# Seven fast products in another order, one block load fewer for each, and the short chunk second

## The reference

```python
h = rmsnorm(x, attn_norm)
proj = einsum('bsd,de->bse', h, w_in)          # 4352 columns
out_a = dilated_attention(qa, ka, va, slopes_a)
out_b = swa_sink_attention(qb, kb, vb, slopes_b, sinks)
mix = concatenate([rmsnorm(out_a, out_norm_a), rmsnorm(out_b, out_norm_b)], axis=-1)
x = x + einsum('bse,ed->bsd', mix, w_out)
h = rmsnorm(x, ffn_norm)
gate = einsum('bsd,df->bsf', h, w_gate)        # 5632 columns
up = einsum('bsd,df->bsf', h, w_up)
x = x + einsum('bsf,fd->bsd', silu(gate) * up, w_down)
return rmsnorm(x, final_norm)
```

## The kernel before

| product | weight operand | made in |
|---|---|---|
| P1 | near left | y, loaded |
| P5 | near right - near left | x = x - y (DVE, `f_sum`) |
| P6 | far right - P5's | x = z - x (`f_sum`) |
| P7 | far right - near right | y = z - y (`f_sum`), after y was loaded with near right a second time |
| P3 | far right | z |
| P4 | P6's operand - far left | x = x - z (`f_sum`), after z was loaded with far left |
| P2 | far left | z |

## Time and profile before

### The profile page before, as it was taken

How to read it: one execution, slowest core, us unless ns; L and a number is a source line. 1 busy time by engine, 2 the same in 40 slices (tenths; PEclk the granted TensorE clock), 3 DMA queues, 4 the chain that set the end, 5 groups by cost and what they waited for, 6 DMA issues and landing times.

```text
span 2030.3 us, 29105 instructions
## 1 busy us (share of the span) xinstructions
PE 1956.6 (96%) x10132; PEld 1668.6 (82%) x10132; DVE 1736.3 (86%) x2397; ACT 1258.9 (62%) x2238; POOL 169.2 (8%) x261
## 2 busy tenths in 40 slices
PE   9999999999999999999999999999997998999984
PEld 8888888888888988888888888888885776777763
DVE  8877677777767999999999999999997979879878
ACT  6566666675346555555555555555566887888864
POOL 4012323223000000000000000000000000000000
PEclk9999999999999999999999999999998999999987
DMA  9322222224334344444444444444465564464542
GB/s 341 119 84 74 68 69 72 69 73 151 94 114 155 127 136 135 135 135 135 131 139 135 136 135 135 135 135 135 135 223 181 187 218 141 150 222 150 168 145 83
DMA packets 133626, 279.30 MB, mean 138 GB/s; under 512 B 12592, under 2 KB 12624, under 8 KB 132608
## 3 DMA queue, kind: packets, MB, share of 16 engines
q1 hardware_dynamic: 121488, 242.27, 37.5%
q0 software_dynamic: 6640, 23.82, 3.0%
q10 hardware_dynamic: 5376, 11.56, 1.6%
HBM read 246.14 MB, written 31.46 MB: 137 GB/s over the span
## 4 chain that ended last, share of the span: by engine, by line
PE 75%; DVE 15%; DMA 4%; issue 3%; ACT 2%; SPq 0%; POOL 0%; ACTq 0%; POOLq 0%; DVEq 0%
PE bank L841 24%; PE bank L844 13%; PE bank L702 8%; PE bank L704 8%; PE bank L703 8%; DVE f_lo L1688 5%; DMA fast_z<-in_w_down 3%; PE bank L768 3%; PE bank L770 3%; PE bank L769 3%; PE bank L894 1%; DVE fast_y L2210 1%; DVE fast_x L2207 1%; DVE a_lo L1688 1%; PE bank L879 1%
## 5 line engine op out<-in xcount | busy, mean ns | idle before, releaser
L841 PE MATMUL bank<-s_two,t_hi 128*128 128x512 f32 x2352 | 557.3, 390 | 0.0
L1428 ACT ACTIVATE t_hi<-t_raw 128x1792 fp32r<-128x1792 f32 x176 | 302.7, 1721 | 360.4 <-DVE t_raw L2056 272.8
L841 PEld LDWEIGHTS bank<-s_two,t_hi 128*128 128x128 f32 x2352 | 433.5, 188 | 84.7
L2062 DVE TENSOR_TENSOR t_lo<-t_raw,t_hi 128x1792 fp32r<-128x1792 f32 x176 | 355.3, 2019 | 20.7 <-ACT t_hi L1428 20.1
L844 PEld LDWEIGHTS bank<-s_two,t_lo 128*128 128x128 f32 x2352 | 298.9, 191 | 10.6 <-DVE t_lo L2062 0.8
L844 PE MATMUL bank<-s_two,t_lo 128*128 128x256 f32 x2352 | 302.3, 283 | 0.4 <-DVE t_lo L2062 0.4
L702 PE MATMUL bank<-f_hi,a_hi 128*128 128x512 f32 x616 | 250.7, 407 | 52.2 <-DVE f_lo L1688 45.6
L703 PE MATMUL bank<-f_hi,a_lo 128*128 128x512 f32 x616 | 246.0, 399 | 0.0
L704 PE MATMUL bank<-f_lo,a_hi 128*128 128x512 f32 x616 | 245.8, 399 | 0.0
L2053 DVE TENSOR_TENSOR t_raw<-t_raw 128x1024 f32<-128x1024 f32 x176 | 214.7, 1220 | 19.2 <-DMA t_raw<-in_w_gu 17.5
L702 PEld LDWEIGHTS bank<-f_hi,a_hi 128*128 128x128 f32 x616 | 119.1, 193 | 92.6 <-DVE f_lo L1688 63.9
(11 more groups left out here) (233 smaller groups left out, 3413.5 us busy)
## 6 DMA issues: line engine op xcount, KB each, us to landing
t_raw<-in_w_gu SPq DMA_DIRECT2D x348, 256.0 KB, 2.8
raw<-in_w_in SPq DMA_DIRECT2D x104, 256.0 KB, 2.6
fast_y<-in_w_down SPq DMA_DIRECT2D x44, 512.0 KB, 4.4
fast_z<-in_w_down SPq DMA_DIRECT2D x44, 512.0 KB, 5.5
gu_mid<-part POOLq DMA_DIRECT2D x43, 512.0 KB, 2.9
...
```

The source lines that it names most:

```text
L841: mm = nc.tensor.matmul(b[:, :], t_hi[r][:, ti, q, :], both, start=d == 0 and q == 0, stop=d == DOUBLES - 1 and q == 1 and i < 4, skip_gro ...
L1428: nc.scalar.activation(t_hi[r][:, :, :, :].rearrange("p a q c -> p (a q c)"), t_raw[r][:, 1:8, :, :].rearrange("p a q c -> p (a q c)"), AC ...
L2062: nc.vector.tensor_tensor(t_lo[r][:, :, :, :].rearrange("p a q c -> p (a q c)"), t_raw[r][:, 1:8, :, :].rearrange("p a q c -> p (a q c)"), ...
```

## The change

The products P6 and P7 change places, so the order is P1, P5, P7, P6, P3, P4, P2, and the buffers are used so that each of the four blocks is loaded once:

| product | weight operand | made in |
|---|---|---|
| P1 | near left | y, loaded |
| P5 | near right - near left | y = x - y |
| P7 | far right - near right | x = z - x |
| P6 | far right - P5's | y = z - y |
| P3 | far right | z |
| P4 | P6's operand - far left | y = y - x, after x was loaded with far left |
| P2 | far left | x |

The load of far left into x is issued when `f_low` of P7 is done. The next chunk's blocks are issued after P3 (z), P4 (y) and P2 (x). The short chunk becomes the second (`DEPTHS = (2, 1, 2, 2, 2, 2)`), and the start and the end of the stage are rewritten for this: more tiles are gated before and in the first slots, the sums of group 43 (`post(7, 1)`) move from slot 1 to slot 4, the residual is loaded after the last chunk's P6 rather than in its P3, and its first add stands in slot 16.

The diff without the places of buffers and the counts that follow from the new order:

```diff
-P1, P5, P6, P7, P3, P4, P2 = range(FAST)
-SUMMED_W, SUMMED_A = (P5, P6, P7, P4), (P5, P6, P7, P3)
-FAST_FROM = "yxxyzxz"
+P1, P5, P7, P6, P3, P4, P2 = range(FAST)
+SUMMED_W, SUMMED_A = (P5, P7, P6, P4), (P5, P7, P6, P3)
+FAST_FROM = "yyxyzyx"
 FAST_BANK = (((0, 4), (6, 1)), ((2, 3), (5, 7)))
 CHUNKS = 6
 ENDING = CHUNKS - 1
-DEPTHS = (1,) + (2,) * ENDING
+DEPTHS = (2, 1, 2, 2, 2, 2)
...
+    def follows(c, u):
+
+        return min((d for d in range(c + 1, CHUNKS) if DEPTHS[d] > u), default=CHUNKS)
...
         sp.wait_ge(t_used, ALL_T - 3)
-        for k in (0, 1, 4, 5):
-            sp.wait_ge(gu_stored, 16 * (tile_of(0, k) + 1))
+        for k in range(2):
             load_gu(0, k)
         sp.wait_ge(t_used, ALL_T - 2)
         for h in range(2):
             load_block("y", 0, 0, h, 0, 0)
+        for k in (2, 3):
+            load_gu(0, k)
         sp.wait_ge(t_used, ALL_T - 1)
         for h in range(2):
+            load_block("y", 0, 1, h, 0, 0)
+        for k in (4, 5):
+            load_gu(0, k)
+        for h in range(2):
             load_block("x", 0, 0, h, 0, 1)
+        for k in (6, 7):
+            load_gu(0, k)
+        sp.wait_ge(t_used, ALL_T)
         for h in range(2):
-            load_block("z", 0, 0, h, 1, 1)
-        for k in (4, 5, 6, 7, 2, 3):
-            sp.wait_ge(gu_stored, 16 * (tile_of(1, k) + 1))
-            load_gu(1, k)
+            load_block("x", 0, 1, h, 0, 1)
+        for u in range(2):
+            for h in range(2):
+                load_block("z", 0, u, h, 1, 1)
         for v in range(len(UNITS)):
             c, p, u, h = UNITS[v]
             e = v - FIRST_UNIT[c]
-            if p == P5:
-                sp.wait_ge(f_lo_done, UNIT_AT[c, P1, u, h] + 1)
-                sp.wait_ge(f_sum_done, W_SUM[c, p, u, h])
-                load_block("y", c, u, h, 0, 1)
-            if p == P3:
+            if p == P7:
                 sp.wait_ge(f_lo_done, v + 1)
-                load_block("z", c, u, h, 1, 0)
-            if c < ENDING and p == P7:
+                load_block("x", c, u, h, 1, 0)
+            if p == P4 and follows(c, u) < CHUNKS:
                 sp.wait_ge(f_lo_done, v + 1)
-                load_block("y", c + 1, u, h, 0, 0)
-            if c < ENDING and p == P4:
+                load_block("y", follows(c, u), u, h, 0, 0)
+            if p == P2 and follows(c, u) < CHUNKS:
                 sp.wait_ge(f_lo_done, v + 1)
-                load_block("x", c + 1, u, h, 0, 1)
-            if c < ENDING and p == P2:
+                load_block("x", follows(c, u), u, h, 0, 1)
+            if p == P3 and follows(c, u) < CHUNKS:
                 sp.wait_ge(f_lo_done, v + 1)
-                load_block("z", c + 1, u, h, 1, 1)
-            if c == 0 and p == P4:
-                load_block("y", 1, 1, h, 0, 0)
-            if (c, p, h) == (0, P2, 0):
+                load_block("z", follows(c, u), u, h, 1, 1)
+            if (c, e) == (1, 0):
                 sp.wait_ge(gu_stored, 16 * TILES)
-            if c == 0 and p == P2:
-                load_block("x", 1, 1, h, 0, 1)
-            if (c, p, h) == (0, P2, 1):
-                sp.wait_ge(folded, TILES - 2)
-                for half in range(2):
-                    load_block("z", 1, 1, half, 1, 1)
-            if 0 < c < ENDING and e in range(4):
-                before = (c - 1, P2, DEPTHS[c - 1] - 1)
-                sp.wait_ge(a_lo_done, ITEM[before] + 1)
+            if c < ENDING and p == P1 and 4 + e in range(4, 4 + 2 * DEPTHS[c + 1]):
+                sp.wait_ge(gs_done, GATE[c, 5 + 2 * (DEPTHS[c] > 1)])
+                if c > 0:
+                    sp.wait_ge(a_lo_done, ITEM[c - 1, P2, DEPTHS[c - 1] - 1] + 1)
                 load_gu(c + 1, 4 + e)
-            if c < ENDING and p == P7 and h == 1:
-                sp.wait_ge(a_sum_done, A_SUM[c, P7, u])
+            if DEPTHS[c] == 1 and p == P1 and h == 1:
+                for k in (6, 7, 2, 3):
+                    load_gu(c + 1, k)
+            if c < ENDING and p == P6 and h == 1 and u < DEPTHS[c + 1]:
+                sp.wait_ge(a_sum_done, A_SUM[c, P6, u])
                 for k in (2 * u, 2 * u + 1):
                     load_gu(c + 1, k)
-            if (c, p, u, h) == (ENDING, P3, 0, 0):
-                sp.wait_ge(a_sum_done, A_SUM[c, P7, 1])
+            if (c, p, u, h) == (ENDING, P6, 1, 1):
+                sp.wait_ge(a_sum_done, A_SUM[c, P6, 1])
                 sp.wait_ge(a_lo_done, ITEM[c - 1, P2, 1] + 1)
                 for n in range(NC):
                     sp.wait_ge(x_moved[n], X_SPILLED)
...
-            if (c, e) == (ENDING, 17):
-                act.wait_ge(f_lo_done, UNIT_AT[c, P7, 1, 1] + 1)
+            if (c, e) == (ENDING, 21):
+                act.wait_ge(f_lo_done, UNIT_AT[c, P4, 1, 1] + 1)
                 act.dma_start(g_fin[:, :], final_norm.partition_broadcast(P)).then_inc(gfin_loaded, 16)
...
-        f_high(1)
         act.wait_ge(t_lo_done, ALL_T)
         a_high(ITEMS[0])
-        silu(0, 4)
-        silu(0, 5)
-        take_products(7, 1, 0, 5)
+        f_high(1)
+        silu(0, 2)
+        silu(0, 3)
+        take_products(7, 1, 0, 4)
         act.wait_ge(t_used, ALL_T - 1)
         f_high(2)
         a_high(ITEMS[1])
-        take_products(7, 1, 5, QUAD)
+        take_products(7, 1, 4, QUAD)
+        silu(0, 4)
+        silu(0, 5)
...
-                nc.vector.tensor_tensor(x, x, y, ALU.subtract).then_inc(f_sum_done, 1)
+                nc.vector.tensor_tensor(y, x, y, ALU.subtract).then_inc(f_sum_done, 1)
+            elif p == P7:
+                dve.wait_ge(fast_loaded["z", u][h], loads_of("z", c, u, h, 1))
+                nc.vector.tensor_tensor(x, z, x, ALU.subtract).then_inc(f_sum_done, 1)
             elif p == P6:
-                dve.wait_ge(fast_loaded["z", u][h], loads_of("z", c, u, h, 1))
                 dve.wait_ge(f_sum_done, W_SUM[c, P5, u, h])
-                nc.vector.tensor_tensor(x, z, x, ALU.subtract).then_inc(f_sum_done, 1)
-            elif p == P7:
-                dve.wait_ge(fast_loaded["y", u][h], loads_of("y", c, u, h, 2))
                 nc.vector.tensor_tensor(y, z, y, ALU.subtract).then_inc(f_sum_done, 1)
             else:
-                dve.wait_ge(fast_loaded["z", u][h], loads_of("z", c, u, h, 2))
-                nc.vector.tensor_tensor(x, x, z, ALU.subtract).then_inc(f_sum_done, 1)
+                dve.wait_ge(fast_loaded["x", u][h], loads_of("x", c, u, h, 2))
+                dve.wait_ge(f_sum_done, W_SUM[c, P6, u, h])
+                nc.vector.tensor_tensor(y, y, x, ALU.subtract).then_inc(f_sum_done, 1)
...
-            if e == 13:
+            if e == 16:
+                for n in range(NC):
+                    dve.wait_ge(x_moved[n], X_BACK)
+                dve.wait_ge(kept, kept_count(ENDING, P1, 1))
+                for h in range(2):
+                    add_block(sum_of(P1, h), 0, h, r2_sign, 0)
+            if e == 17:
                 dve.wait_ge(kept, kept_count(ENDING, P6, 1))
                 for h in range(2):
                     join(P6, P1, h, 0)
-            if e == 17:
-                dve.wait_ge(kept, kept_count(ENDING, P7, 1))
+            if e == 18:
                 for h in range(2):
                     join(P7, P6, h, h + 1)
-            if e == 18:
-                for h in range(2):
-                    join(P6, P5, h, 2)
...
+            if v in (0, 2):
+                gate_times_up(0, 4 + v)
+                gate_times_up(0, 5 + v)
...
             if v == 1:
+                gate_scaled(0, 6)
+                gate_scaled(0, 7)
+            if v == 4:
                 post(7, 1)
...
+        gate_scaled(0, 2)
+        gate_scaled(0, 3)
+        f_low(1)
+        gate_times_up(0, 2)
+        gate_times_up(0, 3)
+        f_low(2)
+        a_low(ITEMS[1])
         gate_scaled(0, 4)
         gate_scaled(0, 5)
-        f_low(1)
-        gate_times_up(0, 4)
-        gate_times_up(0, 5)
-        f_sum(2)
-        a_sum(ITEMS[1])
-        f_sum(3)
-        f_low(2)
-        a_low(ITEMS[1])
```

More of the change, by code:

```diff
@@ L88 @@
 ENDING = CHUNKS - 1
-DEPTHS = (1,) + (2,) * ENDING
+DEPTHS = (2, 1, 2, 2, 2, 2)
+FIRST_TILE = [4 * sum(DEPTHS[:c]) for c in range(CHUNKS)]
 F_RING, A_RING = 4, 4
@@ L2287, in ending @@
                     add_block(sum_of(P5, h), 1, h + 2, r2_sign, 0)
[L2288 removed]
+            if e == 22:
                 for h in range(2):
                     add_block(sum_of(P6, h), 0, h + 2, r2_sign, 0)
[L2291 to L2293 removed]
             if e == 23:
```

58 lines of the change are left out of this document (29 added, 29 removed).

## The result

The changed kernel takes 2006.57 us (median, 2005.8 to 2007.41, 4 runs) against 2033.16 (2032.0 to 2034.61, 4 runs) of the kernel before on the same chip. The ratio is 0.9869, 95 % interval 0.9852 to 0.9886. The forecast was 2007.0 in a range of 1998 to 2022. In the profiled executions the span falls from 2030.3 to 2005.6 us.

The account below looks back on a forecast made before the run. TensorE, DVE and ACT all near 76 us a middle chunk, with waits on DVE and the far left load; 8.0 - 0.3 + 4.8 + 4.7 + 9.3 = 26.5 us off 2032.1, plus 1.4, gives 2007; range 1998 to 2022.

Parts of the forecast that it names:

- Chunks 3 and 4: Middle chunks: far left load wait gone, DVE's 35.9 us in slots 1 to 11 still cost 3.4; gains 4.8 and 4.7 us.
- Chunk 0: First chunk, now depth 2: DVE's 45.4 us in slots 0 to 11 delay unit 14; 88.7 us, a loss of 12.5.
- Chunk 1: Short chunk: ACT's keeps, seeds and f_high, 3.11 us a slot, exceed TensorE's 2.72; it costs 46.6 us, a loss of 8.5.
- Chunk 2: Chunk behind the short one: starts late with no DVE lead, spending the load's gain; 84.1 us against 83.8.
- 8.5 + 4.2 us: Short chunk's waits: the time that would be saved if ACT's work there were hidden.
- The last chunk: Last chunk: first add at T+49.0, then 37.3 us of dense DVE work to T+89.0; gain 9.3 us.
- Just in time: Last chunk: residual issued in slot 10, T+33.2, lands at T+48, before its first add can start at T+49.0.
- By itself this is worth nothing: Whole down stage: about 11.5 MB less loaded from w_down gains nothing, since the queue is half idle.
- DVE's own wait: Rival, slots 16 to 19: DVE loses what the load lost, chunks 3 and 4 give nothing; 2021 us, chance 0.07.
- The residual late: Rival, last chunk: residual again needs 20 us, landing 4.2 us after the first add could start; 2011 us, chance 0.13.
- The start worse: Rival, stage start: 7 MB of loads behind gate loads and a low clock cost 6 us more; 2013 us, chance 0.13.
- Slower by the clock: Rival, short chunk and next 14 units: a pause before every unit lowers TensorE's clock, costing 31.7 us; 2039, chance 0.08.

Follow-up runs that it names:

- table of two by two: Changed kernel with the far left block issued in slot 5 or 13, four or five loads: chunk 3 takes 79.74 us, but 84.37 with slot 13 and five.

## Why the prediction was right, step by step

The spans differ by 24.7 us where the terms made 26.5. The 1.8 between them are the stage's start (1517.05, not 1515.8: 1.3), chunk 0 (88.97: 0.3), chunk 1 (47.15: 0.55) and chunk 2 (83.78: -0.3). The other traces of kernels with the same work ahead of the stage start it between 1516.1 and 1517.8, so the first is no effect of the change that I could show. That the forecast 2007.0 met the median within 0.4 us is in part luck. The profiled execution was forecast at 2005.6 and took 2007.41, 1.8 us more; to get the median 1.4 us were added, and the median came out 0.8 below the profiled execution, so the two errors cancel.

- **Chunks 3 and 4**, predicted 79.7, measured 79.74 and 79.76. The bound by DVE's 35.9 us in slots 1 to 11 is shown: with four of these gate tiles elsewhere the chunk takes 76.42. The size was right, the reason too narrow. The prediction gave the whole gain to the lead from slot 5 to 16. The table of two by two shows that in the middle chunks it would have been enough to take the four loads of slots 9 to 12 away. The lead is needed in the short chunk, where its loss costs 4.6 us, and in the last, 1.0; the prediction did not say so.
- **Chunk 0**, predicted 88.7. The sum was right in its parts: DVE runs without a wait from 1522.11, T+5.1, to 1567.59, 45.5 us where the sum had 45.4. TensorE lost 1.7 us at units 0 and 1, which the sum did not have, but DVE's queue hides it: in the kernel with the residual at its old place these units lost 0.1 us, and chunk 0 took 88.95 all the same. That group 43's sums and the gate steps are on the path is shown by their removal, 3.7 and 1.8 us.
- **Chunk 1**, predicted 46.6. The seeds and their price are shown (38.96 without them). Waits do not stand ahead of nearly every unit: the first five units run at 2.72 us, since f_high is three slots ahead and this must be used up first. From unit 7 on a pair of units takes 7.8 us.
- **Chunk 2**, predicted 84.1. Unit 45 came at T+9.7 (T+10.1 in the prediction) and unit 14 of the chunk at T+45.6 (T+46.0). "Chunk 2 inherits this" is shown: with ACT's seeds cut in the short chunk and at the start of chunk 2 it takes 80.12. The price that the prediction gave for the seeds, "8.5 + 4.2 us", measures 8.2 + 3.7. Of the second part 1.0 us goes with the short chunk's own seeds and 2.7 only with those of chunk 2's P1 and P5, of which ACT makes three pairs while chunk 1 still runs. Each of these two kernels ran once, so this rests on chunk lengths within a trace, and unchanged chunks agree between traces within 0.1 us.
- **The last chunk**, predicted T+89.0 for the end of slot 25, measured T+89.0. "Just in time" was right for the residual: issued 6.9 us later, at T+40.1, it made DVE wait 5.74, so it has about 1 us to spare. The DMA rates below fall off in the 36th of 40 slices, at 1942.2 or T+45.8, 12.5 us after the first issue, but that is not yet the time at which DVE may go: in the kernel with the late residual they fell off at 1948.3 and DVE was released at 1950.67, 2.3 us later. The same 2.3 us make T+48.1 here, where the prediction had T+48.

The window from 1915.8 to 1945.5 of the changed kernel, GB/s in 40 slices of 0.74 us, the far left blocks first and the residual from the 21st on:

```profile
GB/s 0 72 301 273 83 0 149 303 254 130 262 279 36 30 152 361 163 0 0 0 66 290 408 411 408 400 389 394 381 386 386 392 392 378 386 182 0 0 0 22
```

- **"By itself this is worth nothing"**, of the 11.5 MB: the pages of the two kernels show 246.14 and 234.60 MB read, the 11.5 that were forecast. As bytes they are worth nothing in the middle chunks, as the kernel that loads the block twice shows. Their place is worth something: four loads in slots 9 to 12 ahead of a short lead cost 4.6 us in chunk 3, and four held up ahead of the residual 6.7. What the reload in slots 0 to 3 itself cost no run shows.
- **The rivals.** *DVE's own wait* fell: units 15 to 27 start 2.72 us apart in chunks 3 and 4. *The residual late* fell, with about 1 us to spare. *The start worse* fell by its size. *Slower by the clock* fell: TensorE waits 0.3 to 1.25 us before each of the last seven units of chunk 1 and before six units of chunk 2, and the mean granted clock is 1.00 in both. A pause before every unit, as the rival had it, did not come. The Trainium skill, TensorE: Matmul & The Clock Gate, section A second HAM failure mode, warns of short pauses between groups of matmuls; no trace here shows it for pauses of this size. Longer ones are another matter, as below.
